# A three-layer forward pass on one core: the modulation rows of the opening summed as one of 2048 columns, and the order of the opening's transfers and splits

## The chip, the core and the metric

One core of a Trainium2 chip runs the whole program. TensorE (PE) multiplies into PSUM, which has eight banks of 128x512; ScalarE (ACT), VectorE (DVE) and GpSimd (POOL) work on SBUF and PSUM; SyncE (SP) issues the transfers from HBM. Each engine takes its instructions in the order in which they are written and waits by itself for semaphores. The metric is the device time of one execution in microseconds, lower is better. Before the change it is 2219.57 us (median of 3 runs, 2219.05 to 2219.66).

## The reference, cut to what matters

Activations x (256 rows, 2048 columns) go through a retention block, a latent attention block and a third block with an MLP, all in float32. What the change touches is the modulation in front of the first two, layer 0 and layer 1:

```python
c_act = jax.nn.silu(c)
for i in range(DEPTH):
    mod = (c_act @ ada_w[i] + ada_b[i])[:, None, :]
    shift, scale, gate = jnp.split(mod, 3, axis=-1)
    h = rmsnorm(x, norm_g[i]) * (1.0 + scale) + shift
    ...                       # y = branch(h) starts with h @ w_in
    x = x + gate * y
```

`c_act @ ada_w` has a single row, so it is no matrix product here. `ada_w` comes transposed: for each input block kb of 128 columns of h there are three *rows* (0 shift, 1 scale, 2 gate), each 128 partitions of 2048 numbers, 1 MB. One output column is the sum over a partition of that row times c_act.

## The kernel before, in words

**The stream.** `stream_plan` lays down one list of transfers of 128x1024 (512 KB). An item is a weight block ("w") or half of a modulation row ("adt", layer, kb, row, half). SP issues them in this order (`load`), each into a *lane*: a staging buffer. The first 24 items have 14 lanes (six in `raw`, eight in space that is needed later), from item 24 on there are six. Item n waits until the item that had its lane before has been used. The order in the first phase is: the two rows of kb 0, W0, W1, the two rows of kb 1, W2, W3, and so on to W7; the rest of layer 0's rows lies one half at a time between the weights 8 to 30 and 36 to 58. Layer 0's gate rows and layer 1's rows lie between the weights of the rest of the retention block.

**A weight** is split in two parts of reduced precision: ACT copies it to `whi` (line 1396, `split`), DVE subtracts to `wlo` (line 1722). Only then is its lane free. The parts go to `place(i)`: eight places for the first 80 weights (places 4 to 7 lie in `ahi` and `alo`, so rows of the trace that read `ahi<-raw` and `alo<-raw` are splits too), four later. A weight block then costs 12 matmuls of 128x512 on PE in three products (line 1121, the last of a group line 1147).

**Half a modulation row** is multiplied by `c_wide` (c_act on all partitions) and summed on DVE by one instruction with an accumulated output (line 1729, `adt`) into `sums`. `mods` (lines 1737 to 1742) adds the two halves, the bias and scales by the norm's gain. Then h of that block is modulated on ACT (lines 1410 and 1413, `ahi<-arena`) and its low part made on DVE (line 1768, `alo<-arena`). PE waits for that.

**The opening.** x arrives in four quarters, its squares are summed on ACT and DVE; `norm_diag` puts 1/rms on a diagonal (mean on DVE line 1781, power on POOL line 2181, diagonals on DVE line 1777), and PE turns x by 64 small matmuls with it (line 1197); ACT copies the turned blocks out (line 1400).

**Three phases** take the input blocks 0-3, 4-9 and 10-15. In each, two column groups go side by side (`side_by_side`, two weights for each kb), then the others one after another (`one_group`), 20, 30 and 30 weights. At a group's end four PSUM banks are copied out (`part_out`; the first time by ACT, line 1515, later by DVE, line 1893), and PE needs those banks for a later group.

**What sets the order** on ACT and DVE is `pump`: ahead of block i, `next_block(held)` writes down the loads, splits and sums up to the weight whose place was last used by a block before i - held. So with eight places, and nothing held, the split of weight i + 7 stands ahead of block i. `held` keeps some back, at a group's end, so that they stand behind `part_out`.

Of the kernel before, what the change touches and what calls it, by code (L numbers as in the profile page):

```python
# [114 lines left out]

def stream_plan():
# [36 lines left out]
    due = {}  # L153
    for kbs, first_w, last_w in ((PHASES[1], 8, 30), (PHASES[2], 36, 58)):
        for j in range(24):
            due.setdefault(first_w + j * (last_w - first_w) // 24, []).append((kbs[j // 4], j // 2 % 2, j % 2))
    for i in range(first):
        if i < BESIDE and i % 2 == 0:
            plan += [("adt", 0, i // 2, c, h) for c in range(2) for h in range(2)]
        plan += [("adt", 0, kb, c, h) for kb, c, h in due.get(i, ())]  # L160
        plan.append(w[i])
    ada = [("adt", 0, kb, 2, h) for kb in range(16) for h in range(2)]
    ada += [("adt", 1, kb, c, h) for kb in range(16) for c in range(2) for h in range(2)]
    gate = [("adt", 1, kb, 2, h) for kb in range(16) for h in range(2)]
# [12 lines left out]

def schedule(plan):
# [18 lines left out]
    def pump(upto, stop=None):  # L197
        while at["next"] < (stop or len(plan)) and (stop or at["weight"] <= upto):
# [10 lines left out]
            do("adt", layer, kb, c, h, n)  # L209
            if c == 1 and h and layer == 0 and kb in SINGLE:  # L210
                do("mods", layer, kb, 1)
                ready.append(range(kb, kb + 1))
            elif c == 1 and h and kb % 2:
# [3 lines left out]
            elif c == 2 and h and kb % 4 == 3:  # L217
# [149 lines left out]
    def side_by_side(names, kbs, got):  # L367


        for i, kb in enumerate(kbs):  # L370
            mod_to(kb)
            for name in names:
# [3 lines left out]
                w = next_block(max(0, at["used"] - 2) if kbs[0] == 0 else 0 if i < len(kbs) - 1 else 3)  # L376
# [418 lines left out]
def fused_blocks(nc, ins, out):  # L795
# [5 lines left out]
    with ExitStack() as ctx:  # L801
# [7 lines left out]
        sums = sb("sums", [P, 2, 16, 6])  # L809
# [906 lines left out]
        def vector_program(e):  # L1716
# [7 lines left out]
            def adt(layer, kb, c, h, n):  # L1724
                r, i = raw_of(n), 2 * c + h
                late = layer == 1 and c == 2
                w.wait_ge(*s_raw[lanes[n]].on(n))
                w.wait_ge(*s_act.on("c_late" if late else ("c_wide", 2 * h + 1)))
                e.scalar_tensor_tensor(out=r, in0=r, scalar=1.0, in1=(c_late if late else c_wide)[:, h * 1024:h * 1024 + 1024], op0=ALU.mult, op1=ALU.mult,  # L1729
                                       accum_out=sums[:, layer, kb, i:i + 1]).then_inc(*s_ada.up(("adt", layer, kb, c, h)))  # L1730

            def mods(layer, k0, n):
                ks, last = slice(k0, k0 + n), k0 + n - 1
                o, oa = mod[:, layer, :, ks], mod[:, layer, 1, ks]
                halves = sums[:, layer, ks, 0:4].rearrange("p k (c h) -> p c k h", c=2)
# [8 lines left out]
            def gate_sum(layer, j):  # L1744
# [416 lines left out]
            walk(dict(half_add=half_add, split=split, adt=adt, opening=opening, mods=mods, gate_sum=gate_sum, mod_first=mod_first, norm_diag=norm_diag, half_stat=half_stat, half_diag=half_diag, half_mod=half_mod, half_low=half_low, mod_at=mod_at, split_at=split_at, angles=angles,  # L2161
# [7 lines left out]
        def pool_program(e):  # L2169
# [70 lines left out]
            walk(dict(opening=opening, norm_diag=norm_diag, half_stat=half_stat, rstd=norm_diag, ret_values=ret_values, c_zero=c_zero, c_rstd=c_rstd,  # L2240
# [139 lines left out]
```

## Time and profile before

| | |
|---|---|
| median of 3 runs | 2219.57 us |
| the profiled execution | 2220.38 us, span 2218.6 us |
| PE busy | 2195.9 us (99%), 10264 matmuls |
| DVE busy | 1486.2 us (67%) |
| ACT busy | 1039.9 us (47%) |
| sums of half rows, line 1729 | 184 of 128x1024 in 223.7 us, mean 1218 ns |
| of them after 215 us, until | 888 us |
| transfers | 504.02 MB, mean 227 GB/s |

Times are counted from the span's start. A PE that is busy 99% can be won only where it is idle or slow, so the places of its idle time matter more than the shares. The page's slices show the DMA engines 85 to 95% busy and more in the first 200 us (340 to 374 GB/s in the first slices of 55 us), and about half busy later.

### The profile page before, as it was taken

The page shows a single profiled execution, that of the slowest core. Times are in us where ns is not written, and L with a number is a line of the kernel's source. Part 1 is how long each engine was busy: PE and PEld are TensorE (multiplying, and loading weights), DVE is VectorE, ACT ScalarE, POOL GpSimd, SP SyncE. Part 2 cuts the span into 40 slices and gives each one's busy share as a digit, 9 for nine tenths or more (in the row PEclk, how much of TensorE's full clock was granted, in tenths as well). Part 3 has the DMA queues.
Part 4 walks back from the last instruction along what each step waited for, and adds up shares of the span by engine and source line. Part 5 has one row for each costly group of instructions (what it writes and reads, how often), then busy time and mean ns, then how long its engine had stood idle before and what let it go on. Part 6 is the DMA issues. An engine that isn't in the chain of part 4 may idle for free.

```text
span 2218.6 us, 26728 instructions
## 1 busy us (share of the span) xinstructions
PE 2195.9 (99%) x10264; PEld 1820.4 (82%) x10264; DVE 1486.2 (67%) x1916; ACT 1039.9 (47%) x1358; POOL 87.1 (4%) x72
## 2 busy tenths in 40 slices
PE   7999999999999999999999999999999999999999
PEld 5878778878887878888888888888888888888887
DVE  7989777778787789656775555655555555454554
ACT  5555354444444455545464555445434444344443
POOL 0000000000000000000001100001000000000000
PEclk9999999999999999999999999999999999999999
DMA  9998577978797669645456454555565665666554
GB/s 365 374 340 316 182 279 257 352 281 334 262 334 247 214 246 358 226 126 179 164 177 219 148 185 149 180 187 185 184 194 186 189 191 188 192 187 190 191 188 143
DMA packets 140291, 504.02 MB, mean 227 GB/s; under 512 B 15714, under 2 KB 16514, under 8 KB 139394
## 3 DMA queue, kind: packets, MB, share of 16 engines
q1 hardware_dynamic: 139808, 502.09, 66.5%
q8 instruction: 81, 1.33, 0.2%
q14 instruction: 48, 0.39, 0.1%
q10 hardware_dynamic: 354, 0.22, 0.0%
HBM read 500.13 MB, written 2.11 MB: 226 GB/s over the span
## 4 chain that ended last, share of the span: by engine, by line
PE 94%; DVE 3%; DMA 2%; ACT 1%; issue 0%; SPq 0%; POOL 0%; DVEq 0%; ACTq 0%
PE ps L1121 76%; PE ps L1147 8%; PE ps L1213 3%; PE ps L1161 2%; DMA raw<-in_ret_in 1%; DVE raw L1729 1%; DVE wlo L1722 1%; PE ps L1314 0%; DMA raw<-in_ada_t 0%; PE ps L1292 0%; PE ps L1291 0%; PE ps L1240 0%; PE ps L1197 0%; DVE alo L1722 0%; PE ps L1349 0%; PE ps L1297 0%
## 5 line engine op out<-in xcount | busy, mean ns | idle before, releaser
L1722 DVE TENSOR_TENSOR wlo<-raw,whi 128x1024 fp32r<-128x1024 f32 (+1 forms) x711 | 863.4, 1220 | 560.1 <-ACT whi L1396 557.3
L1396 ACT ACTIVATE whi<-raw 128x1024 fp32r<-128x1024 f32 (+1 forms) x711 | 740.1, 1045 | 810.7 <-PE ps L1121 625.7
L1121 PE MATMUL ps<-whi,ahi 128*128 128x512 f32 x2466 | 782.1, 397 | 3.7 <-ACT arena L1515 3.7
L1121 PE MATMUL ps<-wlo,ahi 128*128 128x512 f32 x2466 | 766.1, 391 | 0.5 <-DVE wlo L1722 0.5
L1121 PE MATMUL ps<-whi,alo 128*128 128x512 f32 x2466 | 765.9, 391 | 0.0
L1121 PEld LDWEIGHTS ps<-wlo,ahi 128*128 128x128 f32 x2466 | 463.4, 188 | 99.2 <-DVE wlo L1722 1.2
L1121 PEld LDWEIGHTS ps<-whi,alo 128*128 128x128 f32 x2466 | 463.4, 188 | 97.0
L1121 PEld LDWEIGHTS ps<-whi,ahi 128*128 128x128 f32 x2466 | 454.3, 189 | 95.5 <-issue 4.7
L1729 DVE SCALAR_TENSOR_TENSOR raw<-raw,arena 128x1024 f32<-128x1024 f32 x184 | 223.7, 1218 | 0.0
L1147 PE MATMUL ps<-whi,ahi 128*128 128x512 f32 x254 | 99.6, 392 | 0.0
L1147 PE MATMUL ps<-wlo,ahi 128*128 128x512 f32 x254 | 99.0, 390 | 0.0
L1147 PE MATMUL ps<-whi,alo 128*128 128x512 f32 x254 | 98.9, 389 | 0.0
L1213 PEld LDWEIGHTS ps<-ident,arena 128*128 128x128 f32 x498 | 61.0, 139 | 14.3
L1213 PE MATMUL ps<-ident,arena 128*128 128x128 f32 x498 | 72.3, 272 | 0.0
L2238 POOL TENSOR_TENSOR arena<-arena 128x512 f32<-128x512 f32 x32 | 43.9, 1399 | 560.5 <-ACT arena L1707 560.5
L1396 ACT ACTIVATE ahi<-raw 128x1024 fp32r<-128x1024 f32 x38 | 39.9, 1061 | 49.5 <-DMA raw<-in_ret_in 40.0
L1848 DVE SCALAR_TENSOR_TENSOR alo<-ps,ahi 128x512 fp32r<-128x512 f32 x45 | 31.1, 691 | 45.5 <-ACT ahi L1492 45.5
L1492 ACT ACTIVATE ahi<-ps 128x512 fp32r<-128x512 f32 x45 | 26.8, 596 | 72.5 <-PE ps L1213 72.5
L1147 PEld LDWEIGHTS ps<-wlo,ahi 128*128 128x128 f32 x254 | 47.7, 188 | 9.9
L1147 PEld LDWEIGHTS ps<-whi,alo 128*128 128x128 f32 x254 | 47.7, 188 | 9.7
L1147 PEld LDWEIGHTS ps<-whi,ahi 128*128 128x128 f32 x254 | 47.7, 188 | 9.6
L1722 DVE TENSOR_TENSOR alo<-raw,ahi 128x1024 fp32r<-128x1024 f32 x38 | 46.0, 1222 | 9.2 <-ACT ahi L1396 9.0
(225 smaller groups left out, 1319.4 us busy)
## 6 DMA issues: line engine op xcount, KB each, us to landing
raw<-in_mlp SPq DMA_DIRECT2D x256, 512.0 KB, 4.0
raw<-in_ret_in SPq DMA_DIRECT2D x188, 512.0 KB, 5.2
raw<-in_ada_t SPq DMA_DIRECT2D x184, 512.0 KB, 5.2
raw<-in_in SPq DMA_DIRECT2D x80, 512.0 KB, 4.4
raw<-in_ret_out SPq DMA_DIRECT2D x64, 512.0 KB, 4.7
raw<-in_mla_in SPq DMA_DIRECT2D x48, 512.0 KB, 4.7
raw<-in_mla_out SPq DMA_DIRECT2D x32, 512.0 KB, 4.1
raw<-in_out SPq DMA_DIRECT2D x32, 512.0 KB, 3.6
```

Source lines behind the costliest of these rows:

```text
L1121: mm = e.matmul(acc_[:, :], (ahi, alo, ahi)[m][:, slot, kb, tb * P:(tb + 1) * P], parts[m][:, chunk(n)], start=first and m == 0, stop=False)
L1147: mm = e.matmul(ps[bank[0]][:, :], (ahi, alo, ahi)[m][:, slot, kb, tb * P:(tb + 1) * P], parts[m][:, chunk(n)], start=False, stop=end and ...
L1161: mm = e.matmul(acc_[:, c % 2 * 256:c % 2 * 256 + 256], ws[:, c * P:(c + 1) * P], xs, start=first and m == 0 and c % 2 == 0, stop=end and ...
L1213: mm = e.transpose(acc_[:, i * P:(i + 1) * P], s, ident[:, :])
L1396: e.activation(high(i)[:, 0:ncol], raw_of(n)[:, 0:ncol], ACT.Copy).then_inc(*s_hi.up(i))
L1492: e.activation(at_pair(slot, kb0)[0], ps[bank[0]][:, :], ACT.Copy).then_inc(*s_ahi.up((src, kb0 + 1)))
L1722: e.tensor_tensor(low(i)[:, 0:ncol], raw_of(n)[:, 0:ncol], high(i)[:, 0:ncol].bitcast(F32), ALU.subtract).then_inc(*s_lo.up(i))
L1729: e.scalar_tensor_tensor(out=r, in0=r, scalar=1.0, in1=(c_late if late else c_wide)[:, h * 1024:h * 1024 + 1024], op0=ALU.mult, op1=ALU.mu ...
L1848: e.scalar_tensor_tensor(out=lo, in0=ps[bank[0]][:, :], scalar=1.0, in1=hi.bitcast(F32), op0=ALU.mult, op1=ALU.subtract).then_inc(*s_at.up ...
L2238: e.tensor_tensor(o, o, o, ALU.mult).then_inc(*s_pool.up(("u", g, n, tb)))
```

## The change

- `adt` sums both halves of a row in one instruction of 2048 columns. It waits for both transfers and needs them in two lanes side by side; `add_rows` puts the row in front of the last weight where the lanes would not be neighbours. So all rows of layer 0, and shift and scale of layer 1, go whole; the gate rows of layer 1 stay halves (`late_sum`).
- `sums` has one number for a row, so `mods` loses its first addition; for a single kb it is two instructions, shift and scale, and the first needs only row 0.
- `ROWS`: row (1, 0), the first of input block 1, comes ahead of W0; likewise (2, 0) ahead of W2 and (3, 0) ahead of W4.
- The opening: the mean stands ahead of the first row's sum (`rstd_first`), the diagonals behind it; two turns on PE and ACT come before the modulation of block 0, six behind the split of W0 and W1.
- `HELD`: how many weights are held back at a group's end, in one step for each of the last calls. Side by side: before 3 in the last two calls of phases two and three, now 1, 2, 3 in the last three of phase two and 1, 2 in phase three. One group: before 2 in the last call, now 1 in phase one, 1 and 2 in phase two, 1, 2 and 3 in phase three.

The diff, without what only follows from this:

```diff
+ROWS = (((0, 0), (0, 1), (1, 0)), ((1, 1), (2, 0)), ((2, 1), (3, 0)), ((3, 1),))
+HELD = {0: (None, 1), 4: (3, 2), 10: (2, 3)}
...
+def add_rows(plan, layer, kb, c):
+
+    at = len(plan) - (lane_of(len(plan)) == RAW - 1 and plan[-1][0] == "w")
+    assert lane_of(at + 1) == lane_of(at) + 1, at
+    plan[at:at] = [("adt", layer, kb, c, h) for h in range(2)]
...
-        for j in range(24):
-            due.setdefault(first_w + j * (last_w - first_w) // 24, []).append((kbs[j // 4], j // 2 % 2, j % 2))
+        for j in range(12):
+            due.setdefault(first_w + j * (last_w - first_w) // 12, []).append((kbs[j // 2], j % 2))
...
-    pump(0, 3)
-    do("norm_diag", "h0")
+    do("rstd_first")
+    pump(0, 2)
+    do("norm_diag")
+    pump(0, 4)
+    for k2 in range(2):
+        turn_first(k2)
     pump(0, 6)
-    for k2 in range(4):
-        turn_first(k2)
+    mod_to(0)
     pump(0, 8)
-    mod_to(0)
-    for k2 in range(4, 8):
+    for k2 in range(2, 8):
         turn_first(k2)
...
-                w = next_block(max(0, at["used"] - 2) if kbs[0] == 0 else 0 if i < len(kbs) - 1 else 3)
+                left = 2 * (len(kbs) - i) - names.index(name)
+                w = next_block(max(0, HELD[kbs[0]][0] + 1 - left) if kbs[0] else max(0, at["used"] - 2))
...
-            w = next_block(0 if i < len(kbs) - 1 else 2)
+            w = next_block(max(0, HELD[kbs[0]][1] + 1 - len(kbs) + i))
...
-            def adt(layer, kb, c, h, n):
-                r, i = raw_of(n), 2 * c + h
-                late = layer == 1 and c == 2
+            def adt(layer, kb, c, n):
+                r = raw_of(n, 2)
                 w.wait_ge(*s_raw[lanes[n]].on(n))
-                w.wait_ge(*s_act.on("c_late" if late else ("c_wide", 2 * h + 1)))
-                e.scalar_tensor_tensor(out=r, in0=r, scalar=1.0, in1=(c_late if late else c_wide)[:, h * 1024:h * 1024 + 1024], op0=ALU.mult, op1=ALU.mult,
-                                       accum_out=sums[:, layer, kb, i:i + 1]).then_inc(*s_ada.up(("adt", layer, kb, c, h)))
+                w.wait_ge(*s_raw[lanes[n + 1]].on(n + 1))
+                w.wait_ge(*s_act.on(("c_wide", 3)))
+                e.scalar_tensor_tensor(out=r, in0=r, scalar=1.0, in1=c_wide, op0=ALU.mult, op1=ALU.mult,
+                                       accum_out=sums[:, layer, kb, c:c + 1]).then_inc(*s_ada.up(*[("adt", layer, kb, c, h) for h in range(2)]))
...
-                e.tensor_tensor(o, halves[:, :, :, 0], halves[:, :, :, 1], ALU.add).then_inc(*s_vec.up(("mod red", layer, last)))
-                w.wait_ge(*s_vec.on(("mod red", layer, last)))
-                w.wait_ge(*s_pool.on("one more"))
-                e.tensor_tensor(o, o, ada_bias(layer)[:, 0:2, ks], ALU.add).then_inc(*s_vec.up(("mod sum", layer, last)))
+                w.wait_ge(*s_pool.on("one more"))
+                if n == 1:
+                    w.wait_ge(*s_ada.on(("adt", layer, k0, 0, 1)))
+                    e.tensor_tensor(mod[:, layer, 0, ks], summed[:, 0, :], ada_bias(layer)[:, 0, ks], ALU.add).then_inc(*s_vec.up(("shift", layer, k0)))
+                    w.wait_ge(*s_ada.on(("adt", layer, k0, 1, 1)))
+                    e.scalar_tensor_tensor(out=oa, in0=summed[:, 1, :], scalar=ada_bias(layer)[:, 1, ks], in1=col("norm_g", layer * 16 + k0), op0=ALU.add, op1=ALU.mult
+                                           ).then_inc(*s_vec.up(("mod", layer, k0)))
+                    return
```

**The opening on DVE.** `L1762` and `L1799` close the sum of squares; `L1729` and `L1751` are the sums of rows, `L1781` and `L1818` the mean, `L1777` and `L1814` the diagonals that PE waits for, `L1737` to `L1742` and `L1768`, `L1770` the modulation. Before:

```order
L1762 TENSOR_REDUCE stat<-stat 128x2 [waits scalar_result,vector_result]
L1729 SCALAR_TENSOR_TENSOR raw,sums<-raw,arena 128x1024 [waits raw_landed0]
L1729 SCALAR_TENSOR_TENSOR raw,sums<-raw,arena 128x1024 [waits scalar_result,raw_landed1]
L1729 SCALAR_TENSOR_TENSOR raw,sums<-raw,arena 128x1024 [waits raw_landed2]
L1781 TENSOR_SCALAR stat<-stat 128x2 [waits vector_result]
L1777 TENSOR_SCALAR dg<-ident,stat 128x128 [waits pool_result,ident_landed]
L1777 TENSOR_SCALAR dg<-ident,stat 128x128
L1729 SCALAR_TENSOR_TENSOR raw,sums<-raw,arena 128x1024 [waits raw_landed3]
L1737 TENSOR_TENSOR mod<-sums 128x2 [waits ada_sums]
```

Now:

```order
L1799 TENSOR_REDUCE stat<-stat 128x2 [waits scalar_result,vector_result]
L1818 TENSOR_SCALAR stat<-stat 128x2 [waits vector_result]
L1751 SCALAR_TENSOR_TENSOR raw,sums<-raw,arena 128x2048 [waits scalar_result,raw_landed1,raw_landed0]
L1814 TENSOR_SCALAR dg<-ident,stat 128x128 [waits pool_result,ident_landed]
L1814 TENSOR_SCALAR dg<-ident,stat 128x128
L1751 SCALAR_TENSOR_TENSOR raw,sums<-raw,arena 128x2048 [waits raw_landed3,raw_landed2]
L1768 TENSOR_TENSOR mod<-sums,cols 128x1 [waits ada_sums]
L1770 SCALAR_TENSOR_TENSOR mod<-sums,cols 128x1 [waits ada_sums]
L1751 SCALAR_TENSOR_TENSOR raw,sums<-raw,arena 128x2048 [waits raw_landed5,raw_landed4]
```

The mean moved ahead of the first row; the diagonals, before behind three halves, stand behind one whole row; and a third row (raw_landed4 and 5, kb 1) stands where the first weight's low part was.

**ACT at the end of the second phase's side by side groups.** `L1396` and `L1418` are splits of weights, the last four being W33 to W36 before and W32 to W35 now; `L1515` and `L1537` copy eight banks out of PSUM. Before:

```order
L1396 ACTIVATE whi<-raw 128x1024 [waits weight_products,raw_landed5]
L1396 ACTIVATE whi<-raw 128x1024 [waits weight_products,raw_landed0]
L1396 ACTIVATE whi<-raw 128x1024 [waits weight_products,raw_landed1]
L1396 ACTIVATE ahi<-raw 128x1024 [waits weight_products,raw_landed4]
L1515 ACTIVATE arena<-ps 128x512 [waits weight_products] x8
L1396 ACTIVATE ahi<-raw 128x1024 [waits raw_landed0]
```

Now:

```order
L1418 ACTIVATE whi<-raw 128x1024 [waits weight_products,raw_landed4]
L1418 ACTIVATE whi<-raw 128x1024 [waits weight_products,raw_landed5]
L1418 ACTIVATE whi<-raw 128x1024 [waits weight_products,raw_landed0]
L1418 ACTIVATE whi<-raw 128x1024 [waits weight_products,raw_landed1]
L1537 ACTIVATE arena<-ps 128x512 [waits weight_products] x8
L1418 ACTIVATE ahi<-raw 128x1024 [waits raw_landed0]
```

The split of W36 (lane 4) stood ahead of the copies; now W36 (lane 0) follows them.

**SP at item 24**, where the lanes go from 14 to six. `later_in` (the last rows) brings small inputs. Before, the items 20 to 28:

```order
L1054 DMA arena<-in_ada_t 128x1024 [waits ada_sums] x2
L1052 DMA arena<-in_ret_in 128x1024 [waits ada_sums] x2
L1054 DMA raw<-in_ada_t 128x1024 [waits ada_sums] x2
L1052 DMA raw<-in_ret_in 128x1024
L1054 DMA raw<-in_ada_t 128x1024
L1052 DMA raw<-in_ret_in 128x1024 [waits weight_low,weight_high]
L1037 DMA arena<-in_pos 128x2
L1038 DMA arena<-in_consts 128x160
L1039 DMA mmask<-in_consts 128x256
```

Now, the items 23 to 29:

```order
L1074 DMA arena<-in_ret_in 128x1024
L1076 DMA raw<-in_ada_t 128x1024 [waits weight_low,weight_high] x2
L1074 DMA raw<-in_ret_in 128x1024 [waits ada_sums]
L1076 DMA raw<-in_ada_t 128x1024
L1076 DMA raw<-in_ada_t 128x1024 [waits ada_sums]
L1074 DMA raw<-in_ret_in 128x1024
L1059 DMA arena<-in_pos 128x2
L1060 DMA arena<-in_consts 128x160
L1061 DMA mmask<-in_consts 128x256
```

Item 24 waited for the sum of a row; now it waits for the split of W4. The second half of a row has no wait of its own, because both lanes come free together.

## Rows read from the trace of the kernel before

**Rows 1.** PE, whole span: line <- releaser: us in total, times, longest.

```profile
PE ps L1121 <- ACT arena L1515: 3.7, 2, 2.8
...
PE ps L1121 <- DVE wlo L1722: 0.5, 1, 0.5
```

**Rows 2.** PE instructions in time, 17 to 130 us: start, us, engine, line.

```profile
17.10 9.30 PE L1197 MATMUL ps<-dg,x 128*128 128x128 f32 x64 [7.41 <-DVE dg L1777]
...
26.16 0.71 PE L1121 MATMUL ps<-whi,ahi 128*128 128x512 f32 x2
...
38.55 0.73 PE L1121 MATMUL ps<-ahi 128*128 128x512 f32 x2 [1.25 <-DVE alo L1768]
...
46.32 0.50 PE L1147 MATMUL ps<-ahi 128*128 128x512 f32 x1 [2.04 <-DVE alo L1768]
...
52.08 0.90 PE L1121 MATMUL ps<-whi,ahi 128*128 128x512 f32 x2
...
75.19 0.89 PE L1121 MATMUL ps<-whi,ahi 128*128 128x512 f32 x2 [0.88 <-ACT arena L1515]
...
118.92 0.39 PE L1147 MATMUL ps<-alo,ahi 128*128 128x512 f32 x1
...
122.12 0.90 PE L1121 MATMUL ps<-whi,ahi 128*128 128x512 f32 x2 [2.82 <-ACT arena L1515]
...
129.48 0.62 PE L1121 MATMUL ps<-whi,ahi 128*128 128x512 f32 x2
129.94 0.62 PE L1121 MATMUL ps<-whi,alo 128*128 128x512 f32 x2
```

**Rows 3.** Instructions in time of DVE, 13 to 17 and 40 to 47 us.

```profile
13.06 1.23 DVE L1729 SCALAR_TENSOR_TENSOR raw<-raw,arena 128x1024 f32<-128x1024 f32 x1
...
16.57 0.48 DVE L1777 TENSOR_SCALAR dg<-ident,stat 128x128 f32<-128x128 f32 x2 [0.92 <-POOL stat L2181]
...
40.70 1.22 DVE L1729 SCALAR_TENSOR_TENSOR arena<-arena 128x1024 f32<-128x1024 f32 x1
...
41.84 1.22 DVE L1729 SCALAR_TENSOR_TENSOR arena<-arena 128x1024 f32<-128x1024 f32 x1
...
43.11 0.16 DVE L1737 TENSOR_TENSOR mod<-sums 128x2 f32<-128x2 f32 x1
...
43.58 2.35 DVE L1722 TENSOR_TENSOR alo<-arena,ahi 128x1024 fp32r<-128x1024 f32 x2
...
45.85 0.42 DVE L1768 TENSOR_TENSOR alo<-arena,ahi 128x256 fp32r<-128x256 f32 x1
```

**Rows 4.** Instructions in time of ACT: W0, W4, W6, W9, W17, W36, W57.

```profile
16.89 1.06 ACT L1396 ACTIVATE whi<-raw 128x1024 fp32r<-128x1024 f32 x1 [6.04 <-DMA raw<-in_ret_in]
...
32.89 1.06 ACT L1396 ACTIVATE ahi<-raw 128x1024 fp32r<-128x1024 f32 x1 [3.02 <-DMA raw<-in_ret_in]
...
40.49 1.06 ACT L1396 ACTIVATE ahi<-arena 128x1024 fp32r<-128x1024 f32 x1 [3.52 <-DMA arena<-in_ret_in]
...
50.39 1.06 ACT L1396 ACTIVATE whi<-raw 128x1024 fp32r<-128x1024 f32 x1 [1.51 <-DMA raw<-in_ret_in]
...
73.50 1.06 ACT L1396 ACTIVATE whi<-raw 128x1024 fp32r<-128x1024 f32 x1 [1.41 <-DMA raw<-in_ret_in]
...
120.44 1.06 ACT L1396 ACTIVATE ahi<-raw 128x1024 fp32r<-128x1024 f32 x1 [3.45 <-DMA raw<-in_ret_in]
...
186.02 1.06 ACT L1396 ACTIVATE whi<-raw 128x1024 fp32r<-128x1024 f32 x1 [2.28 <-DMA raw<-in_ret_in]
```

**Rows 5.** Instructions in time of SP, item 24 of the stream.

```profile
39.66 1.47 SPq L1054 DMA_DIRECT2D raw<-in_ada_t  x2
```

**Rows 6.** Stretch, then busy us (instructions) of each engine, clock, DMA share, GB/s.

```profile
25.00:30.00 5.00, 5.00 (x30) 4.37 (x29) 4.62 (x9) 4.37 (x7) 0.00 (x0) 1.00 1.03 409
...
125.00:130.00 5.00, 5.00 (x20) 4.03 (x19) 3.64 (x5) 3.33 (x4) 0.00 (x0) 0.81 0.90 329
```

**Rows 7.** Waits of all engines, 215 to 2218 us.

```profile
ACT whi L1396 <- PE ps L1121: 625.3, 387, 4.4
```

More of the change, by code:

```diff
@@ L154, in stream_plan @@
     for kbs, first_w, last_w in ((PHASES[1], 8, 30), (PHASES[2], 36, 58)):
-        for j in range(24):
-            due.setdefault(first_w + j * (last_w - first_w) // 24, []).append((kbs[j // 4], j // 2 % 2, j % 2))
+        for j in range(12):
+            due.setdefault(first_w + j * (last_w - first_w) // 12, []).append((kbs[j // 2], j % 2))
     for i in range(first):
         if i < BESIDE and i % 2 == 0:
-            plan += [("adt", 0, i // 2, c, h) for c in range(2) for h in range(2)]
-        plan += [("adt", 0, kb, c, h) for kb, c, h in due.get(i, ())]
+            for kb, c in ROWS[i // 2]:
+                add_rows(plan, 0, kb, c)
+        for kb, c in due.get(i, ()):
+            add_rows(plan, 0, kb, c)
         plan.append(w[i])
-    ada = [("adt", 0, kb, 2, h) for kb in range(16) for h in range(2)]
-    ada += [("adt", 1, kb, c, h) for kb in range(16) for c in range(2) for h in range(2)]
+    ada = [(0, kb, 2) for kb in range(16)] + [(1, kb, c) for kb in range(16) for c in range(2)]
     gate = [("adt", 1, kb, 2, h) for kb in range(16) for h in range(2)]
@@ L208, in pump @@
             _, layer, kb, c, h = plan[n]
-            do("adt", layer, kb, c, h, n)
-            if c == 1 and h and layer == 0 and kb in SINGLE:
+            if layer and c == 2:
+                do("late_sum", kb, h, n)
+            elif h:
+                do("adt", layer, kb, c, n - 1)
+            if not h:
+                continue
+            if c == 1 and layer == 0 and kb in SINGLE:
                 do("mods", layer, kb, 1)
                 ready.append(range(kb, kb + 1))
-            elif c == 1 and h and kb % 2:
+            elif c == 1 and kb % 2:
                 do("mods", layer, kb - 1, 2)
@@ L216, in pump @@
                     ready.append(range(kb - 1, kb + 1))
-            elif c == 2 and h and kb % 4 == 3:
+            elif c == 2 and kb % 4 == 3:
                 do("gate_sum", layer, kb // 4)
@@ L808, in fused_blocks @@
         raw = sb("raw", [P, RAW, 1024])
-        sums = sb("sums", [P, 2, 16, 6])
+        sums = sb("sums", [P, 2, 16, 4])
         whi = sb("whi", [P, RING, 1024], F32R)
@@ L1734, in mods @@
                 o, oa = mod[:, layer, :, ks], mod[:, layer, 1, ks]
-                halves = sums[:, layer, ks, 0:4].rearrange("p k (c h) -> p c k h", c=2)
+                summed = sums[:, layer, ks, 0:2].rearrange("p k c -> p c k")
+                w.wait_ge(*s_pool.on("one more"))
[6 more added lines that the diff above has]
+                    return
                 w.wait_ge(*s_ada.on(("adt", layer, last, 1, 1)))
-                e.tensor_tensor(o, halves[:, :, :, 0], halves[:, :, :, 1], ALU.add).then_inc(*s_vec.up(("mod red", layer, last)))
-                w.wait_ge(*s_vec.on(("mod red", layer, last)))
-                w.wait_ge(*s_pool.on("one more"))
-                e.tensor_tensor(o, o, ada_bias(layer)[:, 0:2, ks], ALU.add).then_inc(*s_vec.up(("mod sum", layer, last)))
+                e.tensor_tensor(o, summed, ada_bias(layer)[:, 0:2, ks], ALU.add).then_inc(*s_vec.up(("mod sum", layer, last)))
                 w.wait_ge(*s_vec.on(("mod sum", layer, last)))
@@ L1747, in gate_sum @@
                 w.wait_ge(*s_ada.on(("adt", layer, 4 * j + 3, 2, 1)))
-                e.tensor_tensor(o, sums[:, layer, ks, 4], sums[:, layer, ks, 5], ALU.add).then_inc(*s_vec.up(("gate_red", layer, j)))
-                w.wait_ge(*s_vec.on(("gate_red", layer, j)))
-                e.tensor_tensor(o, o, ada_bias(layer)[:, 2, ks], ALU.add).then_inc(*s_vec.up(("gate_sum", layer, j)))
+                total = sums[:, layer, ks, 2]
+                if layer:
+                    e.tensor_tensor(o, total, sums[:, layer, ks, 3], ALU.add).then_inc(*s_vec.up(("gate_red", j)))
+                    w.wait_ge(*s_vec.on(("gate_red", j)))
+                    total = o
+                e.tensor_tensor(o, total, ada_bias(layer)[:, 2, ks], ALU.add).then_inc(*s_vec.up(("gate_sum", layer, j)))
             def opening(got):
@@ L1781, in mean, with rstd_first, norm_diag @@
                 e.tensor_scalar(stat[:, o + 10:o + 12], stat[:, o + 8:o + 10], 1.0 / D, EPS, ALU.mult, ALU.add).then_inc(*s_vec.up(("mean", src)))
-            def norm_diag(src):
-                o = SUMS[src]
-                mean(src, o)
+            def rstd_first():
+                mean("h0", SUMS["h0"])
+            def norm_diag():
                 w.wait_ge(*s_in["ident"].on("in"))
-                w.wait_ge(*s_pool.on(("rstd", src)))
+                w.wait_ge(*s_pool.on(("rstd", "h0")))
                 for tb in range(2):
-                    diagonal(src, stat[:, o + 10:o + 12], tb)
+                    diagonal("h0", stat[:, SUMS["h0"] + 10:SUMS["h0"] + 12], tb)
             def half_stat(src, tb):
@@ L2191, in norm_diag, with rstd_first @@
                 power(stat[:, o + 10:o + 12], ("rstd", src))
+            def rstd_first():
+                rstd("h0")
             def half_stat(src, tb):
```

24 lines of the change are left out of this document (15 added, 9 removed).

## The prediction

> **What bounds the kernel now.** I read the busy shares first: PE 99% of the span, so only idle or slow stretches of TensorE can be won. Then its waits [rows 1]: two on ScalarE line 1515 take 3.7 us, VectorE's weight splits 0.5. Then PE in order of time [rows 2], for where they lie: it waits 7.41 before 17.10, 2.04 before 46.32 on the low part of the input and 2.82 before 122.12, and all holes above 1 us lie ahead of 123 us. Dense, it starts a pair of matmuls every 0.454 us (129.48, 129.94, over longer stretches 0.4535). One weight block is six pairs, 2.72 us. I number blocks (and their weights W) by place in the stream: block 0 starts at 26.16, 4 (input block 2) at 38.55, 6 (block 3) at 46.32, 8 at 52.08, 16 at 75.19, 32 at 122.12. Then for each hole what ended it: DVE [rows 3], ACT [rows 4], SP [rows 5], and the DMA rate and clock by stretch [rows 6].
>
> Three limits share the opening. (a) VectorE: input block 2's low part comes out just ahead of 38.55 and block 3's ends at 46.27 [rows 3], PE following at 46.32. (b) Transfers: W0 is the 9th transfer of 512 KB (x's four counted) and landed at 16.89, W4 the 21st at 32.89, W6 the 27th at 40.49 [rows 4], so 1.33 us each, then 1.27. (c) Queueing on ScalarE: the copy out of PSUM at line 1515 stands behind the split of W9 (50.39), W17 (73.50) and W36 (120.44) [rows 4], each begun when its transfer landed; PE goes on 0.62 us after that split ends (50.39+1.06+0.63 = 52.08; 120.44+1.06+0.62 = 122.12).
>
> The last hole is the dearest. The matmul before it starts at 118.92 and the next was due at 119.15, so 2.97 us are idle. From 122.12 to the pair at 129.94 are 13 pairs, 5.90 us dense, and it took 7.82: 1.92 more. In 125 to 130 us the granted clock was 0.81 [rows 6]: part of the stretch at 1.2 GHz, the rest at 2.4, after an idle PE. The hole costs 4.9 us, 2.97 idle and 1.92 slow; a dense PE that did the same work by 129.94 would have begun block 32 at 124.04, and against that I compare.
>
> **The change, part by part.** *The sum.* Two sums of 1024 start 1.14 us apart (40.70, 41.84) [rows 3]. An input part of 256 columns takes 0.42 (45.85) and the sum of 1024 1.22: 768 columns more cost 0.80, so 1024 more cost 1.07. One sum of 2048 is then 1.14 + 1.07 = 2.21, against 2.29 for two. Bounds: 2.13 (2048 columns at 1.04 ns, nothing fixed) and 2.44 (1.22 twice, nothing overlapped). I take 2.21, the value from the rows.
> The Trainium skill (VectorE: DVE Perf Modes, the TRN2 errata) says that an SBUF instruction pays some 150 cycles, 0.16 us, once however long it is. The 1.22 us of one sum fits that, but the next starts 0.08 earlier; by the page each pair would give 0.16, and input block 3 would be ready some 0.6 us earlier than below.
> Its price is latency: it waits for both halves, and both lanes come free after 2.21 instead of one after 1.14.
> *The modulation.* Three operations, 43.11 to 43.58, become two, the first no longer behind the last sum: 0.40 instead of 0.47 to 0.58.
> *The first turn.* Now the mean and the power stand ahead of the row. The second item lands at 13.06; sum to 15.27; the two diagonals take 0.48 and PE starts 0.53 after the first begins (16.57, 17.10): 15.83 instead of 17.10, and block 0 at 24.9 instead of 26.16.
> *Rolled forward* with landings of 1.33, then 1.27, one split on ScalarE 1.06, low part 1.14, and sums 2.21:
> - Row (1,0) lies ahead of W0, so W0 is the 11th, 19.5; its low part is done at 22.4, W1's at 23.5. No wait for PE.
> - Input block 1: row (1,1) landed 23.5, sum 25.7, modulation 26.1, row (2,0) to 28.4, W2, W3 low to 31.1, low part 31.45. PE was due at 30.3. Block 2: 31.5.
> - Input block 2: (2,1) 33.75, modulation 34.2, (3,0) landed 34.2 to 36.45, W4 to 37.65, W5 38.9, low part 39.3. Block 4: 39.35, **0.8 later than before**: the early row now stands ahead of the weights.
> - Input block 3: (3,1) to 41.55, modulation 41.95, W6, W7 to 44.25, low part 44.6; PE is due at 44.95. Block 6: 44.95, 1.4 earlier.
> - Item 24 of the stream (from there only six lanes) was issued at 39.66 [rows 5], when a row sum freed its lane; it now waits for W4's low part, 37.65. So W9, the 34th, has no gap before it: 49.4, split ended 50.45, block 8 at 51.1: 1.0 earlier.
> - W17: before, 16 items after W9, 23.1 us with the small inputs between (50.39 to 73.50). Again 16 items. At that rate 72.5, block 16 at 74.2; at 1.33 an item and 0.7 for the small ones 71.4, and then PE's own 22.1 us from block 8 decide, 73.15. I take 73.9: 1.3 earlier.
> *Held weights.* In the second phase the last three calls side by side now hold 1, 2, 3 instead of 0, 3, 3, so only W35 is split ahead of line 1515. W35 is 30 items behind W17: 72 + 30 x 1.36 = 113, split at 114, while block 31 ends at 73.9 + 16 x 2.72 + 0.3 = 117.8. The first four banks are copied during block 31. So no wait, no slow clock: 117.8 against 124.04, 6.2 us. For W36 nothing is lost: block 36 is 10.9 us further, and it lands near 120. In the first phase's g the last split ahead is W17 before and after, and in the third phase's side by side W66: nothing.
> *What could be late next.* Before, W57's split ended at 187.08 [rows 4] and block 57 was due at 124.04 + 25 x 2.72 = 192.1: 5.0 us spare. PE is 6.2 earlier; the stream is ahead by about 3 at item 80 (120 against 123) and VectorE saves about 1 on rows until W57. Spare: 2.8. It holds, but not by much.
> *Behind the opening* PE is already dense; sums of 1024 become 48 of 2048 until 890 us, beside PE, where ScalarE waits 625 us for PE [rows 7]. Taken at 0, bounds -0.5 and +3.
> Sum: 1.3 + 4.9 = 6.2. The profiled execution took 2220.38, so 2214.2 like for like; the median is 0.8 below it: 2219.57 - 6.2 = **2213.4 us**.
>
> **The rivals.**
> *A, the stream gets slower.* Lanes are held longer (a first half 1.3 + 2.2 us behind its landing, before 1.14). Item n+6 can be asked for 3.5 us after a row's first half and should land at 7.7, so 4.2 us are left, before 5.5; 2.9 us of queued transfers cover it. If they don't, 1.5 us an item: W17 at 74, block 16 at 75.2 or later, weights 19 to 29 paced at 3.0 us a block instead of 2.72, ten blocks, 3 us lost; of the 6.2 remain 1 to 4: 2215.5 to 2218.5. For it: W17 landed only 1.7 us ahead of block 16, and VectorE is 4.62 of 5 us busy with rows and weights mixed [rows 6]. Against: the DMA engines moved 409 GB/s in that same stretch, 25 to 30 us.
> The Trainium skill (DMA: Bandwidth & Descriptors, Specifications) gives a limit of some 358 GB/s of HBM for a core. By it an item takes 1.46 us, W17 lands at 73.5, W35 at 117.4 and the gain is about 4: this rival. The 409 GB/s of the trace speaks against it.
> *B, more than I count.* If 2048 takes less, the landings keep 1.27 and W17 is early, block 8 goes at 50.4 and block 16 at 72.5: 7.6 to 8.5 gained, 2211 to 2212.
> *C, slower.* A row blocks VectorE for 2.21 us at one go, and the splits and copies behind it come up to 1.07 us later. In the rest of the program that is 48 rows. If PE lay on VectorE there, each costs up to 1.07, all 51 us. It cancels the gain at 6 rows, and is slower by over 0.2% from 10; a third of them would give +17, 2230. Against it: PE waits 0.5 us in all for VectorE's weight splits [rows 1], and VectorE itself mostly waits there for ScalarE, which waits for PE [rows 7].
> *D, it doesn't do what it says.* W36's hole closes but one of the same kind opens at another group's end, with the slow clock again: 0 to 2 gained, 2218 to 2219.6.
>
> **How the numbers follow.** Forecast 0.60 (gains 4.8 to 7.4); A 0.17, B 0.11, C 0.06, D 0.06. Runs differ by 0.6 us; 0.2% (4.4 us), about what a measurement can tell, is at 2215.1. Faster: forecast, B and a few hundredths of A, 0.73; slower 0.06 (C); same 0.21. The range 2210.8 to 2218.0 leaves out C, most of D and the end of B.
>
> **What would show it.** Right: the first turn at 15.8; blocks 4 and 6 near 39.4 and 45; block 8 near 51; no PE hole and no clock below 1.00 around 118; sums of 2.2 to 2.3 us. Wrong: a hole at line 1121 on line 1537 (the new number of 1515) or on a weight behind 80 us; fewer than 390 GB/s where it was 410; new waits of PE on VectorE behind 250 us.

## The result, and the profile after

| | before | after |
|---|---|---|
| median of the runs made side by side | 2219.81 us | **2227.54 us** (2224.98 to 2232.31) |
| ratio, 95% interval | | 1.0037 [1.0027, 1.0047] |
| the profiled execution | 2220.38 us | 2229.17 us, span 2227.4 us |

The change costs 7.7 us; the forecast was a gain of 6.2. Outside the range, and on the other side.

The sums of rows among the costliest groups of the page of the kernel after (x how many | busy us, mean ns | idle ahead, what ended it):

```profile
L1751 DVE SCALAR_TENSOR_TENSOR raw<-raw,arena 128x2048 f32<-128x2048 f32 x77 | 176.2, 2288 | 22.3 <-DMA raw<-in_ada_t 22.1
```

77 whole rows, 2288 ns each. Two halves of 1218 ns had taken 2436, so VectorE did get its time back. What is new is at the line's end: the instruction now waits 22.1 us in all for transfers of rows to land, where the half sums of the kernel before show no such wait (0.0). TensorE's waits from 10 to 250 us (engine, what it wrote, line, releaser: us in all, times, longest):

```profile
PE ps L1219 <- DVE dg L1814: 4.8, 1, 4.8
PE ps L1143 <- DVE alo L1805: 3.5, 2, 2.1
PE ps L1143 <- ACT arena L1537: 2.4, 1, 2.4
PE ps L1143 <- ACT whi L1418: 2.0, 2, 1.8
PE ps L1143 <- ACT ahi L1418: 1.8, 2, 1.0
PE ps L1143 <- DVE arena L1931: 1.8, 2, 1.3
```

Against [rows 1] the wait for the copy out of PSUM shrank, and waits for plain weight splits (`whi`, `ahi` at L1418) are there that before did not exist. In order of time (start, duration, the operation, in brackets the idle time ahead of it and what ended it):

```profile
15.41 9.13 PE L1219 MATMUL ps<-dg,x 128*128 128x128 f32 x64 [4.80 <-DVE dg L1814]
31.43 0.73 PE L1143 MATMUL ps<-whi,ahi 128*128 128x512 f32 x2 [1.40 <-DVE alo L1805]
39.31 1.06 PE L1143 MATMUL ps<-ahi 128*128 128x512 f32 x2 [2.14 <-DVE alo L1805]
...
76.60 1.16 PE L1143 MATMUL ps<-whi,ahi 128*128 128x512 f32 x2 [2.42 <-ACT arena L1537]
77.56 1.06 PE L1143 MATMUL ps<-whi,alo 128*128 128x512 f32 x2
78.41 1.06 PE L1143 MATMUL ps<-wlo,ahi 128*128 128x512 f32 x2
...
100.64 0.70 PE L1143 MATMUL ps<-whi,ahi 128*128 128x512 f32 x2 [0.21 <-ACT whi L1418]
112.90 0.70 PE L1143 MATMUL ps<-ahi 128*128 128x512 f32 x2 [0.78 <-ACT ahi L1418]
...
124.20 0.61 PE L1143 MATMUL ps<-whi,ahi 128*128 128x512 f32 x2
...
158.84 1.09 PE L1143 MATMUL ps<-ahi 128*128 128x512 f32 x2 [0.48 <-DVE arena L1931]
181.25 0.73 PE L1143 MATMUL ps<-ahi 128*128 128x512 f32 x2 [1.00 <-ACT ahi L1418]
194.62 0.73 PE L1143 MATMUL ps<-whi,ahi 128*128 128x512 f32 x2 [1.84 <-ACT whi L1418]
214.27 1.09 PE L1143 MATMUL ps<-ahi 128*128 128x512 f32 x2 [1.30 <-DVE arena L1931]
```

Blocks 2 and 4 start where the forecast put them, to 0.1 us. Behind block 4's wait the pairs run at the lower clock, so block 6 starts at 46.48 (forecast 44.95) and block 8 at 51.92 (forecast 51.1), only 0.16 us ahead of before. Block 16 then starts at 76.60 instead of 75.19 [rows 2], not 1.3 earlier. Block 32 starts at 124.20 with no wait ahead of it: the hole that the held weights were to close is closed. But against before this has to be held to 124.04, the dense start worked out in the prediction, so by then nothing is left of the 4.9 us (nor of the opening's 1.3): the wait at 76.60 costs 4.5 us with its slow pairs, where before it cost 1.3, and those at 100.64 and 112.90 another 1.8. Then come four holes where before had none above the profile's limit, 4.62 us of idle time, and 3.0 us more in which pairs start late around them: the same later point of the program (the first matmul with `ident`) is at 219.25 us before and 227.02 after. So the loss arises between 50 and 220 us, in two parts: a gain eaten up to 124 us, and 7.6 us lost behind it. From there to the end of the span it is 1999.4 us before and 2000.4 after, and behind 250 us TensorE waits 1.4 us in all in both.

Not all four holes are the rows' doing. Those at 158.84 and 214.27 wait for a copy out of PSUM (line 1931) and cost 3.1 us with their late pairs; the run e1 below, without whole rows, has two of the same kind that cost as much. The two that wait for weight splits, 181.25 and 194.62, cost 4.0 us and are not in e1.

Why the splits are late is seen in the stream. Two stretches (window, its length, then the busy us of TensorE, its weight loads, VectorE, ScalarE and GpSimd, then granted clock, DMA share and GB/s), before:

```profile
50.00:120.00 70.00, 68.40 (x298) 55.21 (x296) 62.62 (x91) 38.99 (x49) 0.00 (x0) 1.00 0.99 376
120.00:205.00 85.00, 82.88 (x358) 68.33 (x359) 75.30 (x109) 43.56 (x54) 0.00 (x0) 0.98 0.96 353
```

and after:

```profile
50.00:120.00 70.00, 66.56 (x280) 52.89 (x279) 55.97 (x59) 37.52 (x48) 0.00 (x0) 0.98 0.95 342
120.00:205.00 85.00, 81.41 (x352) 65.23 (x351) 71.93 (x80) 40.97 (x52) 0.00 (x0) 1.00 0.92 332
```

376 became 342 GB/s though the same items are asked for; VectorE has more idle time, so it isn't the limit. SP's queue after (start, time, line, what it issues), the sum of a row on VectorE, and ScalarE's splits in the same stretch:

```profile
94.00 0.80 SPq L1074 DMA_DIRECT2D raw<-in_ret_in  x2
95.18 1.90 SPq L1076 DMA_DIRECT2D raw<-in_ada_t  x2
98.77 0.81 SPq L1074 DMA_DIRECT2D raw<-in_ret_in  x2
```

```profile
91.67 2.28 DVE L1751 SCALAR_TENSOR_TENSOR raw<-raw,arena 128x2048 f32<-128x2048 f32 x1
```

```profile
92.59 1.06 ACT L1418 ACTIVATE ahi<-raw 128x1024 fp32r<-128x1024 f32 x1 [2.09 <-DMA raw<-in_ret_in]
93.87 1.06 ACT L1418 ACTIVATE ahi<-raw 128x1024 fp32r<-128x1024 f32 x1 [0.22 <-DMA raw<-in_ret_in]
99.43 1.06 ACT L1418 ACTIVATE whi<-raw 128x1024 fp32r<-128x1024 f32 x1 [4.50 <-DMA raw<-in_ret_in]
```

The sum of 91.67 to 93.95 gave two lanes back at once, and SP issued two transfers together at 94.00; the first of them landed just ahead of the split at 99.43, 5.4 us after its issue. Between, ScalarE had nothing to split for 4.50 us. In the kernel before SP issues one at a time, a weight and half a row in turn, 1.1 to 1.2 us apart, and in 90 to 105 us no split waits longer than 2.38 us:

```profile
92.73 0.33 SPq L1052 DMA_DIRECT2D raw<-in_ret_in  x1
93.83 0.33 SPq L1054 DMA_DIRECT2D raw<-in_ada_t  x1
95.01 0.33 SPq L1052 DMA_DIRECT2D raw<-in_ret_in  x1
```

What SP waits for, 40 to 210 us, before:

```profile
SPq L1054 <- DVE raw L1729: 36.8, 35, 2.2
SPq L1052 <- DVE raw L1729: 12.9, 14, 2.0
```

and after:

```profile
SPq L1074 <- DVE raw L1751: 44.0, 19, 4.0
SPq L1076 <- DVE raw L1751: 16.2, 5, 4.6
```

Half as many waits for a sum, each twice as long and longer.

### The profile page after: what moved, and what is told of

It is laid out like the page before. It is cut to its first block, busy times and chain, and to the rows that moved or that the text cites. A ratio compares the mean times of both kernels' runs of the same rounds, so it can differ in the third digit from the quotient of the medians.

```text
span 2227.4 us, 26623 instructions
## 1 busy us (share of the span) xinstructions
PE 2200.3 (99%) x10264; PEld 1819.3 (82%) x10264; DVE 1478.3 (66%) x1733; ACT 1039.1 (47%) x1358; POOL 91.4 (4%) x72
## 4 chain that ended last, share of the span: by engine, by line
PE 89%; DMA 5%; DVE 4%; ACT 1%; issue 1%; SPq 0%; DVEq 0%; ACTq 0%
PE ps L1143 72%; PE ps L1169 8%; PE ps L1235 3%; DMA raw<-in_ada_t 3%; DMA raw<-in_ret_in 2%; PE ps L1183 2%; DVE raw L1751 2%; DVE wlo L1744 1%; PE ps L1336 0%; PE ps L1314 0%; PE ps L1313 0%; PE ps L1262 0%; PE ps L1371 0%; PE ps L1319 0%; ACT ahi L1418 0%
## 5 line engine op out<-in xcount | busy, mean ns | idle before, releaser
L1418 ACT ACTIVATE whi<-raw 128x1024 fp32r<-128x1024 f32 (+1 forms) x709 | 737.7, 1045 | 809.6 <-PE ps L1143 564.5
L1751 DVE SCALAR_TENSOR_TENSOR raw<-raw,arena 128x2048 f32<-128x2048 f32 x77 | 176.2, 2288 | 22.3 <-DMA raw<-in_ada_t 22.1
L1418 ACT ACTIVATE ahi<-raw 128x1024 fp32r<-128x1024 f32 x38 | 39.9, 1058 | 56.4 <-DMA raw<-in_ret_in 47.9
L1886 DVE SCALAR_TENSOR_TENSOR alo<-ps,ahi 128x512 fp32r<-128x512 f32 x45 | 31.1, 691 | 45.9 <-ACT ahi L1514 45.9
```

The lines of the kernel that those rows point to most:

```text
L1418: e.activation(high(i)[:, 0:ncol], raw_of(n)[:, 0:ncol], ACT.Copy).then_inc(*s_hi.up(i))
L1751: e.scalar_tensor_tensor(out=r, in0=r, scalar=1.0, in1=c_wide, op0=ALU.mult, op1=ALU.mult, accum_out=sums[:, layer, kb, c:c + 1]).then_inc ...
L1886: e.scalar_tensor_tensor(out=lo, in0=ps[bank[0]][:, :], scalar=1.0, in1=hi.bitcast(F32), op0=ALU.mult, op1=ALU.subtract).then_inc(*s_at.up ...
```

## The experiments

The theory of the lanes: with six lanes the stream lives on how soon each is given back; a whole row starts late (it waits for its second half) and gives both lanes back late and together. Its rivals: the long instruction on VectorE itself, the new order of the opening, the held weights. In "e1" to "e9" the ratio is against the kernel before, run on the same chip between them.

**e1_halves_beside.** The kernel after, whose pairs of halves stay neighbours in the stream, but each half is summed by its own instruction and gives its own lane back:

```diff
-                r = raw_of(n, 2)
-                w.wait_ge(*s_raw[lanes[n]].on(n))
-                w.wait_ge(*s_raw[lanes[n + 1]].on(n + 1))
+                for h in range(2):
+                    r = raw_of(n + h)
+                    w.wait_ge(*s_raw[lanes[n + h]].on(n + h))
```

> The changed kernel, but each row is summed by two instructions of 1024 columns, each starting when its own half has landed and giving its own lane back. Order of transfers, held weights and opening stay as changed. Theory 1 (a row of 2048 keeps two of six lanes until its end, and the stream of transfers starves): most of the loss goes, 2213 to 2217 us, and item 75 (W35) lands by 114 us instead of 120.8. Theory 2 (the order is at fault: two halves back to back delay the splits of weights behind them): still 2224 to 2230 us, the splits as late as now.

Measured 2215.7 us, 0.9984 [0.9975, 0.9994]: 3.7 us faster than before, 11.8 less than the kernel after. The stream is back at 379 GB/s from 50 to 120 us:

```profile
50.00:120.00 70.00, 70.00 (x308) 57.36 (x307) 63.29 (x92) 42.93 (x57) 0.00 (x0) 1.00 1.00 379
```

TensorE is busy for all 70 us. So the row summed as one, with what that does to the lanes, carries the loss, not the order of the stream. The 11.8 us compare medians of different sets of runs; each against its own runs of the kernel before, it is 7.7 + 3.7 = 11.4.

**e2_rows_only.** The other side: the kernel after with the opening and the held weights of before.

```diff
-ROWS = (((0, 0), (0, 1), (1, 0)), ((1, 1), (2, 0)), ((2, 1), (3, 0)), ((3, 1),))
+ROWS = tuple(((kb, 0), (kb, 1)) for kb in range(4))
...
-            w = next_block(max(0, HELD[kbs[0]][1] + 1 - len(kbs) + i))
+            w = next_block(0 if i < len(kbs) - 1 else 2)
```

> Of the change only the rows of 2048 with their adjacent transfers and shorter modulation; the order of the opening (row (1,0) behind W0 and W1, the mean behind the first row, four turns then four) and the held weights as before. Theory 1: the whole loss is here, 2226 to 2233 us, with the hole at 119 us of before still there. Theory 3 (the early rows ahead of the weights and the slow clock after their hole cost it): 2218 to 2221 us.

2229.11 us, 1.0043 [1.0029, 1.0057]. Whole rows alone cost 9.7 us. Its holes at the copies out of PSUM:

```profile
77.09 1.19 PE L1141 MATMUL ps<-whi,ahi 128*128 128x512 f32 x2 [3.11 <-ACT arena L1535]
...
128.67 1.19 PE L1141 MATMUL ps<-whi,ahi 128*128 128x512 f32 x2 [5.06 <-ACT arena L1535]
```

The hole of 2.82 at 122.12 [rows 2] has become one of 5.06 at 128.67, since W36's split comes 6.5 us later (126.98 against 120.44).

**e3_held_only** and **e4_opening_only.** The kernel before with `HELD` alone, and with the order of the opening alone (`ROWS`, the mean ahead, two turns ahead of block 0; halves throughout). The edits are those of the diff further up.

> The kernel before with the new numbers of held weights alone. Theory 1 and the forecast's term for the hole at 119 us: it closes, no slow clock behind it, 2219.6 - 4.9 = 2214.7 us (2213.5 to 2216). If the stream had no room for it (the rival): 2218 to 2220 us, with a hole elsewhere.

> The kernel before with the new order of the opening alone: mean first, two turns then six, rows (1,0), (2,0), (3,0) ahead of W0, W2, W4, all as halves of 1024, held weights as before. Theory 1: block 0 at 24.9 us, block 4 near 39.4, block 8 near 51, then W17 and W36 gate as before: 2218 to 2220 us. Theory 3: slower, 2222 us or more, by a hole and a slow clock at 36 to 42 us.

2217.34 us, 0.9989 [0.9979, 0.9998], and 2218.15 us, 0.9994 [0.9985, 1.0004]. The held weights gain 2.1 us, the opening 1.3, an amount that its interval does not tell from none. For e3 that misses the expectation of 2213.5 to 2216 us. In the profile of e3 the hole at 122 is gone, the one of block 16 is still there, and one wait is new:

```profile
74.24 0.90 PE L1124 MATMUL ps<-whi,ahi 128*128 128x512 f32 x2 [0.70 <-ACT arena L1518]
...
202.81 1.10 PE L1124 MATMUL ps<-ahi 128*128 128x512 f32 x2 [1.16 <-DVE arena L1896]
```

The second is the copy out of PSUM by VectorE at a later group's end, the forecast's rival D, small. It takes back 1.2 us of the 4.9, and 1.8 with the two late pairs around it.

**e5_start_late** and **e6_release_late.** Both are e1 with one half of the suspicion added. In e5 the first half also waits for the second to land; in e6 SP waits with the first half's lane until the second's sum is done.

```diff
+                    w.wait_ge(*s_raw[lanes[n]].on(n))
+                    w.wait_ge(*s_raw[lanes[n + 1]].on(n + 1))
```

```diff
-                    w.wait_ge(*s_ada.on(plan[m]))
+                    w.wait_ge(*s_ada.on(plan[m] if plan[m][1:4:2] == (1, 2) else plan[m][:4] + (1,)))
```

> As e1 (two instructions of 1024 for a row, the rest as changed), but the first also waits until the second half has landed; each lane is still given back by its own instruction. Theory 1a (the loss is that a lane is held while the other half is still on its way, up to 1.3 us): about half of the 11.8 us between e1 (2215.7) and the changed kernel (2227.5), 2220 to 2223 us. Theory 1b (the loss is the late and common release of both lanes): 2215 to 2218 us, like e1.

> As e1, each half summed as soon as it lands, but the transfer that takes over the first half's lane waits for the second half's sum too. Theory 1a: 2215 to 2219 us. Theory 1b: 2221 to 2228 us. If neither e5 nor e6 is slower than 2219 us, the single long instruction itself (VectorE blocked for 2.2 us) would be at fault.

2217.18 us, 0.9994 [0.9985, 1.0004], and 2224.69 us, 1.0026 [1.0015, 1.0037]. Starting late costs 1.5 us over e1 (their intervals overlap, so it may be less), giving back late and together 9.0; the whole row, which does both, 11.8. The 1.3 us that are left belong to the two together or to the long instruction itself; no run tells which. In e6 no instruction on any engine is longer or more than in e1, only SP's wait is another, and the stream falls from 379 to 357 GB/s, with the same kind of holes:

```profile
50.00:120.00 70.00, 68.79 (x296) 54.64 (x295) 60.05 (x86) 40.12 (x53) 0.00 (x0) 1.00 0.97 357
```

```profile
97.40 0.70 PE L1143 MATMUL ps<-whi,ahi 128*128 128x512 f32 x2 [0.45 <-ACT whi L1418]
109.28 0.70 PE L1143 MATMUL ps<-ahi 128*128 128x512 f32 x2 [0.42 <-ACT ahi L1418]
...
188.94 0.73 PE L1143 MATMUL ps<-whi,ahi 128*128 128x512 f32 x2 [0.66 <-ACT whi L1418]
```

**e7_whole_outside.** e1 again, with whole rows only for items before 24 (14 lanes) and from 144 on (behind the opening phases), where transfers are not short. The second of such a row's two numbers is a zero, set at the start.

```diff
+                if n < 24 or n >= 144:
+                    r = raw_of(n, 2)
...
+                e.memset(sums[:, :, :, :], 0.0).then_inc(*s_pool.up("no sums"))
```

> As e1, but the rows of the first 24 items (14 lanes) and those behind the opening (item 144 on) are one instruction of 2048; only the rows of the six-lane stretch of the opening stay two of 1024. Theory 1: as fast as e1, 2214 to 2217 us, since lanes are short only in that stretch. The rival of slower rows behind the opening (the forecast's case C): 2220 us or more.

2215.66 us, 0.9985 [0.9975, 0.9994], the same as e1. Whole rows are free where lanes are plenty, and behind the opening the long instruction delays nothing: no trace of rival C. Nor do they gain anything there, since VectorE's time isn't wanted.

**e8_all_but_whole.** The kernel before with opening order, `ROWS` and `HELD`, halves spread singly as before.

> The kernel before with the new opening order and the new held weights, the halves of rows one at a time between the weights as before, three short operations for the modulation. Theory 1: at least as good as e1 and better than e3 (2217.3) and e4 (2218.2) alone, 2213 to 2216 us. If the two parts gain nothing together (the stream of transfers decides): 2216 to 2218 us.

2215.68 us, 0.9985 [0.9976, 0.9995]. e1, e7 and e8 agree; all three beat both kernels, by 0.15% the kernel before. The two gains add up to 3.4 by e3 and e4, and 3.4 to 3.7 is measured.

**e9_five_lanes.** To weigh the lanes by themselves: the kernel before, with five from item 24 on.

```diff
-            return n % EARLY if n < 24 else (n - 24 + 24 % EARLY) % RAW
+            return n % EARLY if n < 24 else (n - 20) % 5
```

> The kernel before with five lanes instead of six from item 24 on, nothing else. Lane theory (a transfer takes 5.2 us and more from issue to landing in the stream, whatever is queued, so a lane's period is that plus the wait for its split and the split): six lanes gave 1.36 us an item, a period of 8.2 us; five would give at best the same period, 1.64 us an item, some 0.27 us more for each of the 70 items of the first 120 us behind item 24, where VectorE or TensorE don't bound it: W36's split some 12 to 18 us later than 120.44, under 330 GB/s in 50 to 120 us, and 2235 to 2260 us in all. Rival (the time to landing is mere queueing behind the other transfers, so that with fewer in flight each lands sooner and the DMA engines stay as busy): five in flight of 1.25 us each are still enough, W36 within 3 us of before and the time within 4 us of before's.

2236.07 us, 1.0076 [1.0059, 1.0093]: 16.7 us slower, within what the lane theory gave and far from its rival's 4. But two of its numbers missed. The stream made 344 GB/s from 50 to 120 us, not under 330, and W36's split came at 126.29, 5.9 later and not 12 to 18. Lines of its DMA view from 50 to 200 us bear on why (MB, mean GB/s; then for the weights the median us from issue to landing; the rows' is the same):

```profile
DMA packets 13837, 50.46 MB, mean 336 GB/s; under 512 B 1538, under 2 KB 1538, under 8 KB 13829
...
raw<-in_ret_in SPq DMA_DIRECT2D x52, 512.0 KB, 5.3
```

In the kernel before the same view reads:

```profile
DMA packets 14907, 54.32 MB, mean 362 GB/s; under 512 B 1653, under 2 KB 1670, under 8 KB 14898
...
raw<-in_ret_in SPq DMA_DIRECT2D x61, 512.0 KB, 5.7
```

With one lane fewer each lands 0.4 us sooner, so a part of the 5.7 us is queueing, as the rival had it: taking a sixth of the lanes took only 7% of the rate. How large a part, the page of the kernel before bounds. `in_out` is issued one transfer about every 3 us, between 1387 and 1477 us, where the DMA share is 0.57:

```profile
raw<-in_out SPq DMA_DIRECT2D x32, 512.0 KB, 3.6
```

So 3.6 us are there nearly without a queue, and at least 2.1 of the 5.7 come with the full stream.

## Why the prediction was wrong

**The step that failed** is the size given to rival A: "4.2 us are left, before 5.5; 2.9 us of queued transfers cover it". On this step the main sum rested too: it let the stream keep its pace ("At that rate 72.5" for W17, 113 for W35) and put the longer hold of the lanes at nothing. From issue to landing a 512 KB transfer takes 5.7 us in that stretch, and the 12 issued between 89 and 105 us in the kernel before took 5.0 to 5.8. 4.2 us could not do. I had taken the transfer for its share of the rate (1.27 us) behind those queued ahead of it, and looked up no issue and its landing in the trace, though the page's DMA issues give that number. The transfer issued at 94.00 in the kernel after shows that it isn't so: the one ahead of it had landed by 96.35, and it took 3.1 us more. The "before 5.5" is a weight's lane (7.7 less 2.2 us of splitting); half a row's had 7.7 - 1.14 = 6.5, so the change took it from above 5.7 to below. And the measured splits: W17's began at 74.92 instead of 72.5, W35's at 120.85 instead of 113.

A balance of the lanes shows the size. Six lanes at 362 GB/s and 0.524 MB an item mean that each lane takes a new item every 8.69 us; less 5.7 to land, it is held 3.0 us by waiting and splitting or summing. After:

```profile
DMA packets 13920, 50.75 MB, mean 338 GB/s; under 512 B 1550, under 2 KB 1551, under 8 KB 13911
...
raw<-in_ret_in SPq DMA_DIRECT2D x54, 512.0 KB, 5.9
raw<-in_ada_t SPq DMA_DIRECT2D x42, 512.0 KB, 5.8
```

that is 9.31 us, of them 3.45 held. A whole row holds its first lane for the second's landing (1.3) and 1.07 more, its second 1.07 more; 42 of 96 items are halves of rows, so by this estimate an item's mean hold grows by 0.44 x (1.3 + 1.07 + 1.07)/2 = 0.75 us, against 0.45 measured; the rest of the 0.62 us by which a lane's round grew is slower landing (5.9 and 5.8 for 5.7). This balance is worked out, e1, e5 and e6 are what shows its cause. From W19 to W29 the stream then took 31.1 us (82.51 to 113.61) where before it took 27.0 (81.24 to 108.27), and TensorE's ten blocks need 27.2: with before's stream the two were level, and every slowing shows at once.

Point by point:
- *The sum of 2048.* Right: from one start to the next it is 2.22 (91.67 to 93.89), 2.29 busy. The Trainium skill's (VectorE: DVE Perf Modes, the TRN2 errata) 150 cycles once for each instruction fits the 2.29 as it fits the 1.22. From start to start a pair saves only 2 x 1.14 - 2.22 = 0.06 us, not the 0.16 of that rule.
- *The opening.* First turn 15.41 (15.83), block 2 31.43 (31.5), block 4 39.31 (39.35). Rolling landings and VectorE's instructions forward works. Missed: behind the idle 2.14 us ahead of block 4 the clock fell, where 2.04 us ahead of 46.32 before had not done it. That makes block 6 46.48 (44.95) and block 8 51.92 (51.1): of the 1.0 us that the opening was to have won by block 8, 0.16 were there.
- *Block 16, 1.3 earlier.* Wrong: 76.60 for 73.9. W17's split began at 74.92 for 72.5, the stream being slower from item 24 on.
- *Held weights, 4.9.* The mechanism was right: no wait at block 32, in the kernel after and in e3. Its gain by itself is 2.1 by the medians, 3.5 between the profiled executions (2216.89 against 2220.38); of the 4.9, 1.8 went into the wait at 202.81 and its late pairs and 0.45 into a pair that starts late at 152.96, which leaves 2.6. The 4.9 were also too much to begin with: their 1.92 us of slow clock belong to the profiled execution. Of the 26 executions of the kernel before that stand beside e3, 14 show a mean granted clock of 0.999 and take 2219.6 us on average, but 9 show 1.000 and take 2218.4; e3 shows 1.000 in 8 of 10.
- *"It holds, but not by much"* (W57). With the stream of e3 it held; with that of after, W57's split came at 194.77 instead of 186.02, and the hole that ends at 194.62 waits for the split just before it, W56's.
- *Rival A* had the mechanism and the place, "weights 19 to 29 paced at 3.0 us a block"; it was 3.1. I had let it cost 3 us in ten blocks and stop. Its waits go on to 194.62 us, while rows are mixed in, and it costs 9.7 to 11.8. My argument against it, 409 GB/s in 25 to 30 us, and the sign "fewer than 390 GB/s where it was 410" came from a stretch whose transfers still had 14 lanes: the kernel after moves 410 there too, and falls from 376 to 342 in 50 to 120 us, where there are six.
- *Rival D* is there in part: two holes at other groups' ends, 0.48 and 1.30 us, without the slow clock; it was to leave a small gain, not a loss.
- *Rival C*, the only one I let end slower, was wrong (e7). A slower case for the opening was missing, though A's own rule, 1.5 us an item, had no reason to end at W29.

By the Trainium skill (DMA: Bandwidth & Descriptors, Anatomy of one DMA, there for GpSimd's path) a transfer costs some 2.0 us and its bytes at 436 GB/s; by that, 3.2 us is an estimate for 512 KB. The trace has 3.6 us for `in_out`, where little else is in flight, and 5.7 to 5.9 in the full stream, from SP's queue. By that rule too the fixed part counts in a lane's round. The 358 GB/s of the Trainium skill (the same title, Specifications), which I had weighed for A, did not bind: e1 held 379 over 70 us. The Trainium skill's section Bandwidth there gives that figure for both cores of a domain streaming, and here one core runs.

## What to carry to other kernels

With few staging buffers a stream's rate is buffers x size / (issue to landing + hold), so read the time from issue to landing in the trace before making anything hold a buffer longer. Merging two operations saves on the engine and pays in buffers: both are given back at the end, together, and giving back late and together is the dear part (9.0 of 11.8 us here). Merge only where buffers are plenty or where the engine's own time is what is waited for.

## What the runs showed of the hardware

- The granted clock falls behind some idle stretches of TensorE and not others of the same length. 2.04 us idle ahead of 46.32 in the kernel before left it at 1.00, and so did 2.50 us in e4, ahead of 118.52; but behind 2.14 ahead of 39.31 and 2.42 ahead of 76.60 in the kernel after the pairs start 0.85 us apart for 3.4 us, nearly twice the dense 0.454, the lower of the two levels (1.2 GHz). The line of e4, and windows of the kernel after:

```profile
118.52 0.90 PE L1125 MATMUL ps<-whi,ahi 128*128 128x512 f32 x2 [2.50 <-ACT arena L1519]
```

```profile
40.00:45.00 5.00, 5.00 (x17) 3.96 (x17) 4.50 (x8) 3.03 (x4) 0.00 (x0) 0.71 0.97 370
75.00:80.00 5.00, 3.40 (x8) 2.63 (x9) 3.71 (x5) 3.87 (x6) 0.00 (x0) 0.71 0.89 307
```

  It isn't the length alone, and executions of one kernel differ in it too (the mean clocks of 0.999 and 1.000 above). What tells them apart I don't know. At 39.31 the 2.14 us idle cost 3.9 with the slow pairs, so I would count a hole of 2 us at up to twice its length.
- The time from issue to landing of one 512 KB transfer is 5.3 us with five lanes and 5.7 with six in the full stream, and 3.6 where one is issued about every 3 us: part of it queueing, the greater part not.
